# Where a round's partial out products stand among the 32x32 products of an 8-round RWKV-7 solve

## What is computed

```python
h = rmsnorm(x, norm1_w) * (1.0 + scale1) + shift1
u = h @ w_in
ym, ... = mamba_ssd_group(u[..., :M_COLS], ...)      # 1024 columns
yr, ... = rwkv7_group(u[..., M_COLS:], ...)          # 16 heads of 64, both directions
mix = concatenate([ym, yr]) @ w_out                  # 2048 x 1024
x = x + gate1 * mix
# then norm, a hierarchical mixture of 32 experts, residual
```

## Time and profile before

| what | us |
|---|---|
| time, median of 3 runs (1186.47 to 1188.67) | 1188.26 |
| span of the profiled execution | 1182.0 |
| TensorE busy in the span | 1113.8 |
| weight loads of TensorE busy | 713.6 |
| VectorE busy | 603.6 |
| ScalarE busy | 323.4 |
| GpSimd busy | 138.7 |

### The profile page before, as it was taken

How to read it: one execution, slowest core, us unless ns; L and a number is a source line. 1 busy time by engine, 2 the same in 40 slices (tenths; PEclk the granted TensorE clock), 3 DMA queues, 4 the chain that set the end, 5 groups by cost and what they waited for, 6 DMA issues and landing times.

```text
span 1182.0 us, 34414 instructions
## 1 busy us (share of the span) xinstructions
PE 1113.8 (94%) x15506; PEld 713.6 (60%) x15506; DVE 603.6 (51%) x1346; ACT 323.4 (27%) x705; POOL 138.7 (12%) x185
## 2 busy tenths in 40 slices
PE   5999999999999899998999999979999999999995
PEld 2655457677765566766667566656585555555543
DVE  0455004667667555766657556642574334344346
ACT  2322111312234254534445354422340000000002
POOL 6000002032003030303303031200000000000001
PEclk9999998999999889999999989989999999999998
DMA  9845643232220121120211101034097999999984
GB/s 330 303 143 186 238 167 83 97 90 72 72 72 1 53 64 40 46 66 20 78 36 52 56 29 49 13 127 113 15 410 290 409 416 416 416 416 415 387 338 161
DMA packets 78945, 200.48 MB, mean 170 GB/s; under 512 B 12628, under 2 KB 21079, under 8 KB 74199
## 3 DMA queue, kind: packets, MB, share of 16 engines
q1 hardware_dynamic: 74816, 186.71, 42.8%
q10 hardware_dynamic: 3127, 8.56, 1.8%
q0 software_dynamic: 864, 3.15, 0.8%
HBM read 186.85 MB, written 11.53 MB: 168 GB/s over the span
## 4 chain that ended last, share of the span: by engine, by line
PE 91%; DVE 3%; issue 3%; ACT 1%; DMA 1%; SPq 0%; DVEq 0%; PEldq 0%; ACTq 0%
PE ps L1663 17%; PE ps L1242 10%; PE ps L1231 7%; PE ps L562 6%; PE ps L625 5%; PE ps L1262 5%; PE ps L1705 4%; PE ps L1899 3%; PE ps L544 2%; PE ps L1621 2%; PE ps L1785 2%; PE ps L1801 2%; PE ps L476 2%; PE ps L594 1%; PE ps L457 1%
## 5 line engine op out<-in xcount | busy, mean ns | idle before, releaser
L1663 PE MATMUL ps<-hT,ring_a 128*128 128x384 f32 x624 | 211.1, 493 | 0.9 <-DVE um_a L2375 0.9
L1663 PEld LDWEIGHTS ps<-hT,ring_a 128*128 128x128 f32 x624 | 117.3, 192 | 80.1 <-issue 5.4
L1231 PE MATMUL ps<-scratch,misc 128*128 128x128 f32 x864 | 99.6, 275 | 1.6 <-DVE misc L2705 1.6
L1231 PEld LDWEIGHTS ps<-scratch,misc 128*128 128x128 f32 x864 | 97.9, 192 | 3.2 <-issue 3.2
L2375 DVE SCALAR_TENSOR_TENSOR um_a<-ps,mum,um_a 128x252 f32<-128x252 f32 (+1 forms) x162 | 57.3, 410 | 66.9 <-ACT um_a L2081 66.0
L562 PEld LDWEIGHTS ps<-ring_a 32*32 32x32 f32 x6144 | 62.1, 105 | 36.9 <-issue 23.6
L1301 ACT ACTIVATE um_a<-ps 128x256 f32<-128x256 f32 x17 | 6.5, 385 | 271.8 <-PE ps L1242 271.8
L562 PE MATMUL ps<-ring_a 32*32 32x32 f32 x6144 | 70.8, 195 | 7.1 <-issue 6.6
L1242 PE MATMUL ps<-ring_a,um_a 128*64 128x512 f32 x288 | 63.4, 593 | 1.5 <-DVE um_a L1283 1.5
L1529 POOL TENSOR_TENSOR mixm<-tri,la 128x512 f32<-128x512 f32 x24 | 28.4, 1208 | 250.9 <-DVE la L2345 165.9
L1242 PE MATMUL ps<-misc,um_a 128*64 128x512 f32 x128 | 56.3, 592 | 1.4 <-DVE um_a L1283 1.4
(11 more groups left out here) (448 smaller groups left out, 2064.8 us busy)
## 6 DMA issues: line engine op xcount, KB each, us to landing
ring_a<-in_w_in SPq DMA_DIRECT2D x10, 2048.0 KB, 8.0
ring_a<-in_w_ada SPq DMA_DIRECT2D x9, 2048.0 KB, 12.3
ring_a<-in_moe_w_gate SPq DMA_DIRECT2D x18, 1024.0 KB, 10.2
ring_a<-in_moe_w_up SPq DMA_DIRECT2D x18, 1024.0 KB, 12.3
ring_a<-in_moe_w_down SPq DMA_DIRECT2D x18, 1024.0 KB, 12.2
ring_a<-in_w_out SPq DMA_DIRECT2D x59, 256.0 KB, 2.8
misc<-in_moe_w_gate SPq DMA_DIRECT2D x16, 512.0 KB, 8.8
misc<-in_moe_w_up SPq DMA_DIRECT2D x16, 512.0 KB, 12.2
```

What stands on the lines that cost most here:

```text
L1231: mm = pe.matmul(ps[:, k // 4, P * (k % 4):P * (k % 4) + P], h2[:, j, P * k:P * k + P], pick[:, j, :], start=(j == 0), stop=(j == NTILE - 1))
L1663: mm = pe.matmul(ps[:, t % 4 if isinstance(t, int) else t, 0:T], slot(n)[:, k, P * c:P * c + P], hT[:, k, :], start=(k == 0), stop=(k == K ...
```

## The change

`partial_at` gets eleven places. In rounds 0 to 5 the products stand at places 0, 2, 4 and 6 (behind the first half of each level), 7 (behind the second half of level 4), 8 (behind the pair products), 9 (behind the half inverse of s = 0) and 10 (behind that of s = 2). Those at places 1, 3 and 5 are gone. Round 6 has places 0, 4, 6, 8, 9 in place of 0, 2, 3, 5, 6, and round 7 is unchanged. ScalarE's copy of bank 7 moves from ahead of the x6 and xT copies to behind the w6 copies, in all rounds.

```diff
         def partial_at(c, i):
 
-            places = {6: (0, 2, 3, 5, 6), 7: (0, 1, 3, 4, 6, 7)}.get(c, tuple(range(8)))
+            places = {6: (0, 4, 6, 8, 9), 7: (0, 1, 3, 4, 6, 7)}.get(c, (0, 2, 4, 6, 7, 8, 9, 10))
             return places.index(i) if i in places else None
...
                 pair_products(pe, s)
+            partial_out(pe, c, 8)
             fill(V_T)
             for s in range(3):
                 pe.wait_ge(inv_j, c * 6 + (s + 1))
                 pe.wait_ge(xT_ok, c * 12 + (9 + s + 1))
                 half_inverses(pe, s)
+                if s != 1:
+                    partial_out(pe, c, 9 + s // 2)
             fill(G_UP)
...
                 prep_act(act, c, 1 - b, V_T)
-            act.wait_ge(half_ps, partial_from(c + 1) if c < 7 else N_PARTIAL)
-            act.activation(half_mix[c], ps[:, 7, :], ACT.Copy).then_inc(half_rd, 1)
             for s in range(3):
                 act.wait_ge(inv_ps, c * 15 + (6 + s + 1))
...
                 act.activation(w6[s].rearrange("p h c -> p (h c)"), ps[:, 2 * s, P:2 * P], ACT.Copy).then_inc(inv_sb, 1)
+            act.wait_ge(half_ps, partial_from(c + 1) if c < 7 else N_PARTIAL)
+            act.activation(half_mix[c], ps[:, 7, :], ACT.Copy).then_inc(half_rd, 1)
```

## The result

| what | before | changed |
|---|---|---|
| median of 9 runs, us | 1188.26 (1185.78 to 1194.44) | 1180.96 (1175.18 to 1186.42) |
| ratio, 95% interval | | 0.9943 [0.9919, 0.9968] |
| span of the profiled execution, us | 1182.0 | 1184.5 |
| time of the changed kernel's profiled execution, us | | 1186.42 |

The change is faster, by 7.3 us between the medians; the prediction was 1183.3. Two repeats on other chips gave 0.9966 [0.9936, 0.9996] and 0.9968 [0.9942, 0.9994], about 4 us.

The account below looks back on a forecast made before the run. TensorE, busy for 1113.8 of 1182.0 us, was taken as the bound, losing time to half clock and instruction stops. Terms of -7.5 - 5.5 + 6.3 + 1.75 = -4.95 us gave 1183.3 us, range 1178.0 to 1191.0.

Parts of the forecast that it names:

- A: The forecast itself: clock holds, stops move from inverse stretch into levels, ScalarE costs a little; 1181 to 1186 us; chance 0.50.
- D: Levels, with fewer wide products, see clock falls themselves and the kernel gets slower; 1191.7 us; chance 0.15.
- Term 1: Inverse stretch (first pair product to first u product): moved wide products keep the clock up, saving 7.5 us.
- Term 2: Inverse stretch (first pair product to first u product): moved products cover instruction stops, saving 5.5 of 6.5 us.
- Term 3: Levels (first blocks_32 to first pair product): less wide work, so more instruction stops, 0.9 us a round, 6.3 us lost.
- Term 4: ScalarE's moved copy of bank 7 makes L855 and u(0) 0.25 us late, 1.75 us lost in seven rounds.
- what lies around it, and that stays: Outside the profiled span: the median of the runs was 6.3 us above the span, expected to stay.

Follow-up runs that it names:

- first repeat: The changed kernel without edit, timed again beside the kernel before on another chip: 1177.38 against 1181.48 us.
- narrow products: The changed kernel with the products at places 8, 9 and 10 computed on 32 rows and 32 columns only: 1216.99 us, ratio 1.0321.
- kernel with products left out: The kernel before with products at places 1, 3 and 5 of rounds 0 to 5 cut to 32x32x32: 1174.96 against 1180.37 us, 0.9951.
- The direct test: The changed kernel with products at places 2, 4, 6 and 7 each cut into four matmuls of 128 columns: 1180.83 against 1184.91 us before.
- kernel with two moved: The changed kernel with bank 7's copy behind the first y_copy and only two products moved in rounds 0 to 5, round 6 re-placed: 1180.16 us, 0.9968 of before.
- changed kernel with round 7 changed too: The changed kernel with bank 7's copy behind the first y_copy and round 7's products at 0, 2, 4, 6, 8, 9: 1174.54 us, 0.9937 of before.

## Why the prediction came out as it did

The direction, the mechanism and the range were right. Of rivals A to D, A came: clock held, stops moved into the levels. Some half clock in levels came with it, as in D, though far less: 3.4 us in round 7 in all three traces and 3.4 more in round 0 in two, which the sum had at nothing. Whether the change causes it is open; the same products with the later copy of bank 7 had neither. Two of the signs named in advance were missed: stops on L575 to L594 were to fall below 2 us and are 3.8, and those on L562 were to rise to about 11 us and are 14.8, 12.2 and 12.1 in the three traces. Term by term:

| term | predicted, us | measured, us | from |
|---|---|---|---|
| 1, clock | -7.5 | -7.4 to -8.9 in the profile, -5.8 to -7.0 over timed executions (estimates) | half clock gone; mean granted clock |
| 2, stops in the inverse stretch | -5.5 | -2.7 (first repeat -3.0) | L575, L579, L594: 6.5 to 3.8 |
| 3, stops in the levels | +6.3 | +9.2 (first repeat +6.6) | L562: 5.6 to 14.8 |
| 4, copy of bank 7 | +1.75 | +0.4 | 0.07 us in six rounds |

- Term 1 held. The narrow products show that it is wide work that keeps the clock up, and the kernel with products left out shows that relief of the levels doesn't. The rule that I had weighed against it, of the Trainium skill ("TensorE: Matmul & The Clock Gate", Part 1), an idle engine at half rate, doesn't account for the fall behind a piece with 3.26 of 3.40 us busy. The consequence that I had drawn from it, a term near 0, did not come.
- Term 2 was mis-sized. The step that failed is "in place of the 8.59 us of work that cover them in round 1 there are then 11.8", which treats cover as if it had to be enough for all stops. Why it wasn't enough is my reading and not tested: the wide products stand at three points, while stops remained at the start of the stretch (1.7 us on L575), where the work ahead of it is the dense 32x32 code of level 4.
- Term 3 was of the right kind and within its upper bound (16.8 us), but on the low side in the profile, +9.2. The step is "I take 0.9": 1.3 a round there, 0.9 in the first repeat. Products left out alone give +6.8 (5.6 to 12.4), so nothing else in the change has to be the cause. The sum under it was too kind as well. The "one packet carries about 270" in it came from 115 packets set against all records, though a packet carries 256. The 1674 instructions of round 1's levels are then 6.5 packets, 23.3 us at 3.56 us each, and the lack against 21.5 is 1.8 us a round instead of 0.6.
- Term 4 was mis-sized. The step is "The copy takes 0.59 us, so L855 comes 0.25 us late, and `u(0)` with it". The first `u` comes only 0.07 us later against L701 than with the copy out of the way. ScalarE's rows of round 1 say why: of two instructions that follow each other at once, the second starts about 0.1 us before the record of the first ends (the exponentials run to 491.88, L858 starts at 491.78). So the copy moved the exponentials back by 0.52 us and not 0.59 (they start 1.23 instead of 0.71 us behind the first w6 copy), and 0.45 us and not 0.34 were free ahead of L855.
- "what lies around it, and that stays", 6.3 us, was wrong. Time around the span is 1.7 to 1.9 us in every execution that lists both. The rest of the gap was that the profiled execution of before was a good one. It did no harm, because the sum was added to the median and not to the span's own time.

With 0.44 us for each us of half clock the terms add up to -2.0 us in the profile, with 0.36 to -0.5, and rounds 0 to 6 did get 1.5 us shorter. The timed runs gained 7.3, 4.1 and 2.5 us between medians. In an average execution the clock's part is -5.8 to -7.0 us; how large the stops are there, no timed run tells. With the first repeat's values, -7.0 - 3.0 + 6.6 + 0.4 = -3.0 (or -1.8), inside that chip's interval (-7.6 to -0.5 us). Why the first comparison gave more than the two others stays open; its interval reaches down to 3.8 us. So part of the closeness of 1183.3 to 1180.96 is luck: terms 2 to 4 were off by 2.8, 2.9 and 1.35 us in the profile, not all the same way, and the chips differ by more than what is left.

That the stops are a lack of instructions was an inference in the prediction, from two stops 3.56 us apart. It is shown by the packets in the section on the profile after: all 381 stops end 1.19 to 1.62 us behind the landing of a packet, and 256 instructions lie between them for each packet. The two packets in question start 3.57 us apart, at 410.18 and 413.75 us. The direct test, more instructions for the same work, came out too small to tell, and the total of 115 packets says nothing for either side, since the instructions are the same. The rule of the Trainium skill ("Runtime: NRT & Kernel Launch", Instruction fetch mechanics) that fetching is hidden isn't true for this code: L562 alone has 15.5 us of such stops in the changed kernel.

## What to carry to other kernels

Wide matmuls that nothing waits for are a means in two ways: placed among small ones they kept the clock at its upper level here, and they give the engine time in which it needs hardly any instructions. Both are used up where they leave, so move the fewest that stop the falls, and read the gain in both stretches. Here one a round did as well as two or three; that it is faster than three isn't shown. Where small matmuls stop on "issue", set the ends of the stops beside the landings of the instruction packets. Where one profile per kernel says the opposite of the timed runs, put its own time beside them and use the mean granted clock of all executions.

## What the runs showed of the hardware

- TensorE ran out of instructions inside dense 32x32 code: 255 to 257 of them from stop to stop, with packets at least 3.2 us apart (a median of 3.87 us in the levels of rounds 1 to 5 of the changed kernel), and a stop ended 1.19 to 1.62 us after a packet's landing.
- Taking 15.8 us of TensorE's busy time out of such code, as 128-row matmuls, saved 5.4 us of the whole. In the levels of rounds 1 to 5, 13.4 us less work made them 6.8 us shorter, and stops of up to 2.0 us took the other half.
- The clock fell behind a piece with TensorE busy for 3.26 of 3.40 us on small tiles alone. It fell in three of seven inverse stretches with narrow products at the new places, and with wide ones in none of seven in the first profile and in one of seven in each repeat. Wide products are no guarantee: round 6 of the kernel with two moved had 10.2 us of half clock with products at places 9 and 10. And the fall at 864.0 us of the changed kernel came behind 3.40 us in which TensorE was busy throughout with 128-row matmuls, of 36 and 128 columns.
- In round 7, with DMA at 0.58 to 0.60 of the stretch, stops were longer: in the changed kernel 2.7 us on L594 and 1.4 on L588. The instruction packet that ended the longer one started 6.4 us after the one before it (784.0 and 790.4 us). That the busy DMA engines held it up is likely and not tested by itself. With two wide products moved there, the stretch took 10.94 us instead of 14.75 before, at full clock and with DMA at 0.43. These are its rows, first of the kernel before:

```profile
784.92:799.67 14.75, 10.48 (x314) 0.66 0.58 216
```

and of the changed kernel with round 7 changed too:

```profile
780.04:790.98 10.94, 9.92 (x316) 1.00 0.43 161
```
